# A three-block float32 network on one core: the turn between sublayers with six held weight units, eight unit buffers and five stream buffers

## The chip, the cores and the metric

The kernel runs on one core of one Trainium2 chip. The metric is the device time of one launch in microseconds (us), as the median of several runs.

## The reference

A residual stream `x` of 256 tokens by 1024 columns, float32, passes two adaLN-modulated blocks and one block of another kind. Cut to what matters:

```
for i in range(2):                       # block i: ffn(i,0), mixer, ffn(i,1)
    mod = silu(c) @ ada_w[i] + ada_b[i]
    x = sub(x, swiglu(ffn_w_in[i,0], ffn_w_out[i,0]))
    x = sub(x, pool_mixer) if i == 0 else sub(x, mla_mixer)
    x = sub(x, swiglu(ffn_w_in[i,1], ffn_w_out[i,1]))
# sub:  h = rmsnorm(x) * g * (1 + scale) + shift;  y = rmsnorm(fn(h)) * g';  x + w * (1 + gate) * y
h = rmsnorm(x)                           # second block
x = x + merged(attention, convolution, memory attention of h @ w_in) @ w_o
x = x + 2 of 32 experts for each token (w_up: 1024 x 512, w_down: 256 x 1024)
```

`swiglu` is `(silu(gate) * up) @ w_out` with `gate, up = h @ w_in` and an inner width of 2816, handled as 11 slices of 256.

## The kernel before, in words

The sublayers have numbers q: 0 is ffn(0,0), 1 the pool mixer, 2 ffn(0,1), 3 ffn(1,0), 4 the MLA mixer, 5 ffn(1,1); then the second block ("mix") and the experts. The 256 tokens are two tiles (t = 0, 1) of 128.

**Weights.** All weights come through one stream. SyncE (`stream`, L430) loads chunks of 1 MB into `NRAW` raw buffers in a fixed order. Chunk m waits until the chunk that lay in its buffer, m - NRAW, is done with: for most chunks until VectorE has split its last unit, for a few that TensorE reads unsplit (`ada_w`, `pool_w` and some of MLA) until TensorE has used them. A chunk has two units of 1024 columns. A unit is split into a high part `uh` (ScalarE, L449) and the rest `ul` (VectorE, L460), kept in `NUNIT` unit buffers; unit u waits until TensorE has used unit u - NUNIT. Both engines take their splits in program order with their other work: `split_high`/`split_low(upto)` emit every split up to a given unit that the raw buffers allow, and whatever is written behind them waits.

**Products.** A float32 product is three matmuls: high by high (L524), rest of the weight (L525), rest of the activation (L526). `linear` goes unit by unit over both tiles. `linear_by_tile` holds `held` units, does all of them for tile 0 and then for tile 1, so that tile 0 is complete earlier; `mid` is put ahead of one unit of tile 0.

**An FFN.** For each slice b, `up(b)` is 48 matmuls into two PSUM banks (banks 4 and 5, `AB`, from b = 1 on), ScalarE takes silu from a bank (`sg`, L1174), VectorE multiplies (`ug`, L1207) and thereby frees the bank, `spread(b)` (L1124) transposes `ug` in the middle of `up(b+1)`, ScalarE and VectorE make its high part and rest (`bh`, `bl`), and `outp(b)` is 24 matmuls into the y banks. The order on TensorE is up(b), outp(b-1), up(b+1), outp(b). In an FFN that ends in a turn, outp(9) and outp(10) are done last and together, by tile. Between these pieces VectorE adds up modulation columns of a later sublayer (L707, L710).

**The turn** (`edge_pe`, `edge_act`, `edge_dve`, `edge_roots_pool`) is used four times: 2 to 3, 3 to 4, 4 to 5, 5 to mix. When y of a tile is complete, VectorE multiplies it by the gain (L1077), ScalarE sums its squares (L802), GpSimd takes the root, VectorE updates x (L1085), ScalarE sums the squares of x, GpSimd takes the root, VectorE makes a diagonal matrix of it (L1091), TensorE multiplies the tile of x by it, which also turns it (L976, 8 matmuls), ScalarE applies scale and shift and rounds (L1038, L1042) and VectorE takes the rest `hl` (L1069), in four groups of 256 columns, g = 0 to 3. Then the first product of the next sublayer starts, by tile, with four units. `keep_busy` (L588) is four matmuls without use.

Of the kernel before, what the change touches and what calls it, by code (L numbers as in the profile page):

```python
# [8 lines left out]
F32R = mybir.dt.float32r  # L9
# [5 lines left out]
P = 128  # L15
T = 2
# [6 lines left out]
NRAW = 6  # L23
NUNIT = 6
# [129 lines left out]
def plan(I):  # L154
# [74 lines left out]
def build(nc, I, out_ap):  # L229
    ctx = ExitStack()  # L230
    with ctx:
# [24 lines left out]
        gT_l = [bl[:, 2 * i:2 * i + 2, :] for i in range(2)]  # L256
        sg = sb("sg", [P, T, 256])
# [294 lines left out]
        def linear_by_tile(pe, key, held, k0, K, lhi, llo, ready, banks, begin=True, mid=None, done=None,  # L552
                           mid_at=None):
# [416 lines left out]
        def edge_turn_pe(pe, q, t):  # L970
            pe.wait_ge(dve_done, tv("dg", q, t))
            for g in range(4):
# [6 lines left out]
                pe.frees(b, act_done, ta, "tf", q, t, g)  # L979
# [30 lines left out]
        def edge_pe(pe, s, q, key, banks, done):  # L1010

            keep_busy(pe, EDGE_BANKS[3], 4)
            edge_turn_pe(pe, q, 0)
            linear_by_tile(pe, key, 4, 0, KD, lh, ll, edge_ready(pe, q), banks,
                           mid=lambda: edge_turn_pe(pe, q, 1), mid_at=3, done=done)

        def edge_act(act, s, q, key, silu, scale, bias, more=True):
# [26 lines left out]

            y_squares(0)
# [20 lines left out]
        def edge_dve(dve, s, q, key, more=True):  # L1066
# [26 lines left out]

            gain(0, 1)
# [12 lines left out]
            low(0, 3)  # L1107
# [10 lines left out]
        def ffn_pe(pe, q, nb, up, down, ready, between, tail=None, begun=False, edge=False):  # L1118
# [10 lines left out]
            def outp(b, mid=None):  # L1129
                n = b % 2  # L1130
                if edge and b == nb - 1:
                    part = lambda v, k, t: v[(b - 1 + k // 2) % 2][:, k % 2, t * P:(t + 1) * P]
                    linear_by_tile(pe, ("fo",), 4, 0, 4, lambda k, t: part(gT_h, k, t),
                                   lambda k, t: part(gT_l, k, t),
                                   lambda k, t: pe.wait_ge(dve_done, tv("gl", q, b - 1 + k // 2)), YB, begin=False,
                                   mid=lambda: spread(b), mid_at=1, done=("y", q))
# [6 lines left out]
            for b in range(nb):  # L1143
# [6 lines left out]
                if b and not (edge and b == nb - 1):  # L1150
                    outp(b - 1, mid=(lambda: spread(nb - 1)) if b == nb - 1 else None)
# [5 lines left out]
        def ffn_act(act, q, nb, up, down, between, tail=None, begun=False, edge=False):  # L1157
            def spread(b):
                act.wait_ge(pe_done, tp("gT", q, b))
                if b >= 2:  # L1160
                    act.wait_ge(pe_done, tp("out", q, b - 2))
                act.e.activation(gT_h[b % 2][:, :, :], PB[6][:, :].rearrange("p (a b) -> p a b", b=S),  # L1162
                                 AF.Copy).then_inc(act_done, ta.put("gh", q, b))

            for b in range(nb):
# [12 lines left out]
                elif b:  # L1178
# [4 lines left out]
            if edge:  # L1183
                held_act(act, ("fo",), 4, 2)
# [3 lines left out]
        def ffn_dve(dve, q, nb, up, down, between, combine=False, tail=None, begun=False, edge=False):  # L1188
            def spread(b):
                n = b % 2  # L1190
# [5 lines left out]
            for b in range(nb):  # L1196
# [14 lines left out]
                elif b:  # L1211
# [4 lines left out]
            if edge:  # L1216
                held_dve(dve, ("fo",), 4, 2)
# [13 lines left out]
        def sub_ffn_pe(pe, i, s, between=nothing, tail=None):  # L1231
# [11 lines left out]
            else:  # L1243
# [3 lines left out]
                   side, tail, begun=q != 2, edge=q > 0)  # L1247
# [23 lines left out]
        def sub_ffn_dve(dve, i, s, between=nothing, tail=None):  # L1271
# [11 lines left out]
            else:  # L1283
                edge_dve(dve, q - 1, q, up_key(i, s)(0))
# [642 lines left out]
        def mla_pe(pe):  # L1927
# [69 lines left out]
            out_unit(2)  # L1997
            three(7)
            for k in range(3, KD - 4):
                out_unit(k)  # L2000
            linear_by_tile(pe, ("mo",), 4, KD - 4, KD, lh, ll, ready, YB, begin=False, done=("y", 4))
            edge_frees(pe, 4)

        def mla_act(act):
# [33 lines left out]
            units_act(act, ("mo",), KD - 4)  # L2038
            held_act(act, ("mo",), 4, 2)

        def mla_dve(dve):
            edge_dve(dve, 3, 4, ("mi",), more=False)
# [41 lines left out]
            units_dve(dve, ("mo",), KD - 4, mid=last_pairs, mid_k=0)  # L2084
            held_dve(dve, ("mo",), 4, 2)
# [542 lines left out]
        def mix_dve(dve):  # L2628
# [7 lines left out]
            for n, (nm, _, _) in enumerate(PROJ):  # L2636
                if n == 0:
                    edge_dve(dve, 5, "mix", ("pj",))
# [808 lines left out]
```

## Time and profile before

| | |
|---|---|
| median of 3 runs | 1566.01 us (1565.28 to 1566.88) |
| profiled execution | 1568.05 us, of which the span of the trace is 1565.8 us |
| mean granted clock of TensorE | 0.993 |
| TensorE busy | 97% of the span |
| VectorE busy | 78% |
| ScalarE busy | 56% |
| GpSimd busy | 7% |
| read from HBM | 371.39 MB |

In a row of a timeline the first number is the start in us from the span's start, the second the duration, "x5" says that five such instructions in a row are shown as one, and a bracket at the end says how long the engine sat idle before and which instruction released it. Matmuls of 512 columns start 0.23 us apart, though each is shown with about 0.39 us, since they overlap.

### The profile page before, as it was taken

What the parts mean: (1) busy time and instruction counts of PE and PEld (TensorE: products, weight loads), DVE (VectorE), ACT (ScalarE), POOL (GpSimd) and SP (SyncE); (2) the same over time, 40 slices, a digit from 0 to 9 for tenths busy, and PEclk for the clock granted to TensorE, in tenths of its full rate; (3) what the DMA queues carried; (4) which work ended last, traced back from release to release, by engine and by line L of the source; (5) the groups of instructions that cost most, each with busy time, mean ns of one, the idle gap of its engine ahead of it and who ended that gap; (6) DMA issues with size and microseconds to landing.
All of it is one profiled execution on the core that took longest, in us unless ns stands there. A gap on an engine that the chain in (4) does not pass through costs nothing.

```text
span 1565.8 us, 19135 instructions
## 1 busy us (share of the span) xinstructions
PE 1520.5 (97%) x7373; PEld 1213.7 (78%) x7373; DVE 1214.8 (78%) x1774; ACT 882.1 (56%) x1357; POOL 115.5 (7%) x176
## 2 busy tenths in 40 slices
PE   6999999999999999999999999999999999999998
PEld 3878876887877887776788887777788888787876
DVE  1898978888867888655586654669888798988996
ACT  3545436544437444476564544655567477776774
POOL 1110020000002000015211000000001000000000
PEclk9999999999999999999999999899999999999999
DMA  9999856998857988333287544445323469989993
GB/s 345 373 378 348 303 206 213 319 315 294 308 173 268 327 295 298 136 109 108 82 295 203 167 163 135 163 143 194 113 89 124 168 248 359 348 315 327 324 338 134
DMA packets 196401, 373.75 MB, mean 239 GB/s; under 512 B 9042, under 2 KB 102672, under 8 KB 196304
## 3 DMA queue, kind: packets, MB, share of 16 engines
q1 hardware_dynamic: 176688, 301.08, 55.7%
q0 software_dynamic: 18928, 69.77, 12.7%
q10 hardware_dynamic: 688, 1.62, 0.3%
q8 instruction: 60, 0.98, 0.2%
q14 instruction: 37, 0.30, 0.1%
HBM read 371.39 MB, written 1.05 MB: 238 GB/s over the span
## 4 chain that ended last, share of the span: by engine, by line
PE 88%; ACT 4%; DVE 4%; DMA 1%; POOL 1%; issue 1%; SPq 0%; DVEq 0%; ACTq 0%
PE banks L524 26%; PE banks L526 25%; PE banks L525 25%; PE banks L1124 1%; ACT arena L802 1%; DVE ul L460 1%; ACT uh L449 1%; PE banks L2361 1%; DMA raw<-in_ffn_w_in 1%; PE banks L2963 1%; PE banks L1970 1%; PE banks L761 1%; ACT full L1038 1%; DMA raw<-in_ada_w 1%; PE banks L1795 1%
## 5 line engine op out<-in xcount | busy, mean ns | idle before, releaser
L460 DVE TENSOR_TENSOR ul<-raw,uh 128x1024 fp32r<-128x1024 f32 (+2 forms) x548 | 656.9, 1209 | 148.9 <-ACT uh L449 139.7
L449 ACT ACTIVATE uh<-raw 128x1024 fp32r<-128x1024 f32 (+2 forms) x548 | 568.4, 1048 | 347.8 <-PE banks L526 341.6
L524 PE MATMUL banks<-uh,hh 128*128 128x512 f32 (+2 forms) x1296 | 517.7, 399 | 13.0 <-DVE hl L1069 6.4
L526 PE MATMUL banks<-uh,hl 128*128 128x512 f32 (+2 forms) x1296 | 504.7, 389 | 0.0
L525 PE MATMUL banks<-ul,hh 128*128 128x512 f32 (+2 forms) x1296 | 503.2, 388 | 0.0
L524 PEld LDWEIGHTS banks<-uh,hh 128*128 128x128 f32 x1296 | 244.8, 189 | 72.2 <-DVE hl L1069 10.1
L526 PEld LDWEIGHTS banks<-uh,hl 128*128 128x128 f32 x1296 | 244.8, 189 | 51.4
L525 PEld LDWEIGHTS banks<-ul,hh 128*128 128x128 f32 x1296 | 245.3, 189 | 45.8 <-issue 0.2
L524 PE MATMUL banks<-uh,bh 128*128 128x512 f32 x512 | 207.2, 405 | 1.0 <-DVE bl L3160 0.9
L526 PE MATMUL banks<-uh,bl 128*128 128x512 f32 x512 | 200.1, 391 | 0.0
L525 PE MATMUL banks<-ul,bh 128*128 128x512 f32 x512 | 199.6, 390 | 0.0
L710 DVE SCALAR_TENSOR_TENSOR arena<-arena,sc 128x512 f32<-128x512 f32 x210 | 157.9, 752 | 9.5
L524 PEld LDWEIGHTS banks<-uh,bh 128*128 128x128 f32 x512 | 96.1, 188 | 29.2 <-DVE bl L3160 6.2
L526 PEld LDWEIGHTS banks<-uh,bl 128*128 128x128 f32 x512 | 96.1, 188 | 20.9
L525 PEld LDWEIGHTS banks<-ul,bh 128*128 128x128 f32 x512 | 96.3, 188 | 20.0 <-issue 1.7
L686 POOL DMA_DIRECT2D arena<-in_ada_w x60 | 45.2, 755 | 480.7 <-DVE arena L710 402.0
L1174 ACT ACTIVATE sg<-banks 128x256 f32<-128x256 f32 x88 | 29.0, 380 | 62.0 <-PE banks L526 62.0
L2344 DVE SCALAR_TENSOR_TENSOR Gs<-arena,Gs 128x256 f32<-128x256 f32 x88 | 42.7, 485 | 3.1
L1207 DVE TENSOR_TENSOR ug<-sg,banks 128x256 f32<-128x256 f32 x88 | 32.9, 414 | 11.4 <-ACT sg L1174 11.4
L1069 DVE TENSOR_TENSOR hl<-full,hh 128x256 fp32r<-128x256 f32 x32 | 13.6, 424 | 27.5 <-ACT hh L1042 27.5
L1192 DVE TENSOR_TENSOR bl<-banks,bh 128x512 fp32r<-128x512 f32 x44 | 30.1, 683 | 4.1 <-ACT bh L1162 4.1
L769 ACT ACTIVATE arena<-banks 128x128 f32<-128x128 f32 x20 | 5.5, 278 | 40.6 <-PE banks L746 40.6
(392 smaller groups left out, 1270.8 us busy)
## 6 DMA issues: line engine op xcount, KB each, us to landing
raw<-in_ffn_w_in SPq DMA_DIRECT2D x176, 512.0 KB, 6.6
raw<-in_w_up SPq DMA_DIRECT2D x64, 1024.0 KB, 7.1
arena<-in_ada_w POOLq DMA_DIRECT2D x60, 1024.0 KB, 6.6
raw<-in_ffn_w_out SPq DMA_DIRECT2D x44, 1024.0 KB, 5.5
raw<-in_w_down SPq DMA_DIRECT2D x32, 1024.0 KB, 7.0
raw<-in_w_in SPq DMA_DIRECT2D x22, 1024.0 KB, 5.0
raw<-in_ada_w SPq DMA_DIRECT2D x12, 1024.0 KB, 11.0
raw<-in_w_mem_kv SPq DMA_DIRECT2D x4, 1024.0 KB, 6.5
```

What stands on the lines that cost most here:

```text
L449: act.e.activation(uh[r][:, 0:w], raw[m % NRAW][:, h * w:(h + 1) * w], AF.Copy).then_inc(act_done, ta.put("hi", u))
L460: dve.e.tensor_tensor(ul[r][:, 0:w], raw[m % NRAW][:, h * w:(h + 1) * w], uh[r][:, 0:w].bitcast(F32), ALU.subtract).then_inc(dve_done, tv. ...
L524: pe.e.matmul(o, a, wh, start=k + j == s0, stop=False)
L525: pe.e.matmul(o, a, wl, start=False, stop=False)
L526: mm = pe.e.matmul(o, b, wh, start=False, stop=k + j == s1)
L686: pool.e.dma_start(ada_raw[m % NADA], v).then_inc(ada_ring[m % NADA], 16)
L710: dve.e.scalar_tensor_tensor(buf, w, sc[:, k:k + 1], buf, ALU.mult, ALU.add).then_inc(dve_done, tv.put())
L761: pe.e.matmul(PB[b], ones[:, :], buf, start=True, stop=True).then_inc(pe_done, tp.put("ada_t", old))
L1174: act.e.activation(sg[:, t, :], PB[up_banks(b)[t]][:, 0:256], AF.Silu).then_inc(act_done, ta.put("silu", q, b, t))
L1192: dve.e.tensor_tensor(gT_l[n][:, :, :], PB[6][:, :].rearrange("p (a b) -> p a b", b=S), gT_h[n][:, :, :].bitcast(F32), ALU.subtract).then_inc(
L1207: mul = dve.e.tensor_tensor(o, sg[:, t, :], u, ALU.mult)
L2344: tap = dve.e.scalar_tensor_tensor(y, u, w, y, ALU.mult, ALU.add)
```

## The change

- `NRAW` goes from 6 to 5, `NUNIT` from 6 to 8.
- In the FFNs that end in a turn (q = 2, 3, 5) outp(8), outp(9) and outp(10) are done last and together, by tile, with six held units. outp(8) no longer stands between up(9) and up(10). The weights stream in that order. Slice 10 has buffers of its own (`ch`, `cl`). In MLA six units instead of four are held for the output product.
- The turn's TensorE work for tile 0 goes ahead of the last held unit of tile 1's y. That for tile 1 goes ahead of tile 1's first product; it stood ahead of tile 0's last unit. `keep_busy` is gone from the turn.
- VectorE takes scale and shift of group 1 of tile 0, and ScalarE's and VectorE's work of the turn is in another order.
- The program is built with a DMA scratch of 4096 bytes (`dynamic_dma_scratch_size=4096`).

```diff
@@
-NRAW = 6
-NUNIT = 6
+NRAW = 5
+NUNIT = 8
@@ the stream's order, ffn(i, s)
-            if b:
+            if b and not (i + s and b >= NFF - 2):
                 wide(("fo", i, s, b - 1), I["ffn_w_out"][i, s], (b - 1) * 256)
-        wide(("fo", i, s, NFF - 1), I["ffn_w_out"][i, s], (NFF - 1) * 256)
+        for b in range(NFF - 3, NFF) if i + s else (NFF - 1,):
+            wide(("fo", i, s, b), I["ffn_w_out"][i, s], b * 256)
@@ linear_by_tile
+                    if late is not None and (t, i) == (1, held - 1 if late_at is None else late_at):
+                        late()
@@ edge_pe
-            keep_busy(pe, EDGE_BANKS[3], 4)
-            edge_turn_pe(pe, q, 0)
-            linear_by_tile(pe, key, 4, 0, KD, lh, ll, edge_ready(pe, q), banks,
-                           mid=lambda: edge_turn_pe(pe, q, 1), mid_at=3, done=done)
+            linear_by_tile(pe, key, 4, 0, KD, lh, ll, edge_ready(pe, q), banks, done=done,
+                           late=lambda: edge_turn_pe(pe, q, 1), late_at=0)
@@ edge_act
+            high(0, 0)
+            second_high()
+            high(0, 2)
             y_squares(1)
-            high(0, 0)
-            high(0, 1)
+            high(0, 3)
             x_squares(1)
-            high(0, 2)
-            high(0, 3)
@@ edge_dve
+            diagonal(0)
+            split_low(dve, dve.unit_at + 3)
+            second_scaled()
+            low(0, 0)
+            low(0, 1)
             gain(1, 1)
-            diagonal(0)
             gain(1, 0)
-            low(0, 0)
+            low(0, 2)
             update(1)
-            low(0, 1)
-            split_low(dve, dve.unit_at + 3)
-            low(0, 2)
+            low(0, 3)
             diagonal(1)
-            low(0, 3)
@@ ffn_pe
-                    linear_by_tile(pe, ("fo",), 4, 0, 4, lambda k, t: part(gT_h, k, t),
+                    linear_by_tile(pe, ("fo",), 6, 0, 6, lambda k, t: part(gT_h, k, t),
...
-                if b and not (edge and b == nb - 1):
+                if b and not (edge and b >= nb - 2):
                     outp(b - 1, mid=(lambda: spread(nb - 1)) if b == nb - 1 else None)
@@ mla_pe
-            out_unit(2)
-            three(7)
-            for k in range(3, KD - 4):
-                out_unit(k)
-            linear_by_tile(pe, ("mo",), 4, KD - 4, KD, lh, ll, ready, YB, begin=False, done=("y", 4))
+            linear_by_tile(pe, ("mo",), 6, KD - 6, KD, lh, ll, ready, YB, begin=False, mid=lambda: three(7), mid_at=1,
+                           done=("y", 4), late=lambda: edge_turn_pe(pe, 5, 0))
```

The order of instructions on two engines, at the places of which the prediction speaks:

On TensorE, sublayer 2, at the end of up(9), before (`uh,bh` is a product with the activations of `outp`, `uh,hh` one of `up`):

```order
L525 MATMUL banks<-ul,hh 128x512
L526 MATMUL banks<-uh,hl 128x512
L524 MATMUL banks<-uh,bh 128x512
L525 MATMUL banks<-ul,bh 128x512
L526 MATMUL banks<-uh,bl 128x512
```

and of the change:

```order
L528 MATMUL banks<-ul,hh 128x512
L529 MATMUL banks<-uh,hl 128x512
L527 MATMUL banks<-uh,hh 128x512
L528 MATMUL banks<-ul,hh 128x512
L529 MATMUL banks<-uh,hl 128x512
```

The first product of up(10) now directly follows the last of up(9); both write banks 4 and 5.

On VectorE, the turn from 2 to 3 from the gain of tile 1 on, before:

```order
L1077 TENSOR_TENSOR arena<-banks,Gs 128x512
L1091 TENSOR_SCALAR arena<-ident,st 128x128
L1077 TENSOR_TENSOR arena<-banks,Gs 128x512
L1069 TENSOR_TENSOR hl<-full,hh 128x2x128
L1085 SCALAR_TENSOR_TENSOR x<-arena,st,x 128x512 x2
L1069 TENSOR_TENSOR hl<-full,hh 128x2x128
L460 TENSOR_TENSOR ul<-raw,uh 128x1024
L1069 TENSOR_TENSOR hl<-full,hh 128x2x128
L1091 TENSOR_SCALAR arena<-ident,st 128x128
L1069 TENSOR_TENSOR hl<-full,hh 128x2x128 x5
L460 TENSOR_TENSOR ul<-raw,uh 128x1024 x5
L1207 TENSOR_TENSOR ug<-sg,banks 128x256 x2
```

and of the change:

```order
L1102 TENSOR_SCALAR arena<-ident,st 128x128
L463 TENSOR_TENSOR ul<-raw,uh 128x1024
L1108 TENSOR_SCALAR full<-banks,ab 128x128 x2
L1080 TENSOR_TENSOR hl<-full,hh 128x2x128 x2
L1088 TENSOR_TENSOR arena<-banks,Gs 128x512 x2
L1080 TENSOR_TENSOR hl<-full,hh 128x2x128
L1096 SCALAR_TENSOR_TENSOR x<-arena,st,x 128x512 x2
L1080 TENSOR_TENSOR hl<-full,hh 128x2x128
L1102 TENSOR_SCALAR arena<-ident,st 128x128
L1080 TENSOR_TENSOR hl<-full,hh 128x2x128 x4
L463 TENSOR_TENSOR ul<-raw,uh 128x1024 x7
L1229 TENSOR_TENSOR ug<-sg,banks 128x256 x2
```

Tile 0's diagonal and first two rests come ahead of tile 1's gain, and seven splits instead of five stand ahead of `ug` of the first slice.

On VectorE, output projection of the second block (the last `hl` are groups 2 and 3 of its input), before:

```order
L2440 TENSOR_TENSOR arena<-arena,banks 128x512 x2
L2445 TENSOR_TENSOR arena<-arena 128x512 x2
L460 TENSOR_TENSOR ul<-raw,uh 128x1024 x6
L853 TENSOR_TENSOR hl<-banks,hh 128x512 x2
L460 TENSOR_TENSOR ul<-raw,uh 128x1024 x3
```

and of the change:

```order
L2460 TENSOR_TENSOR arena<-arena,banks 128x512 x2
L2465 TENSOR_TENSOR arena<-arena 128x512 x2
L463 TENSOR_TENSOR ul<-raw,uh 128x1024 x8
L858 TENSOR_TENSOR hl<-banks,hh 128x512 x2
L463 TENSOR_TENSOR ul<-raw,uh 128x1024 x3
```

Eight splits instead of six stand ahead of the two `hl`. At the start of the experts the same happens ahead of the second expert's `ug` (L3180): seven instead of five.

## Rows read from the trace of the kernel before

**Rows 1.** The page, parts 1 and 6: engine busy us, share, count; DMA issues

```profile
PE 1520.5 (97%) x7373; PEld 1213.7 (78%) x7373; DVE 1214.8 (78%) x1774; ACT 882.1 (56%) x1357; POOL 115.5 (7%) x176
...
raw<-in_w_up SPq DMA_DIRECT2D x64, 1024.0 KB, 7.1
...
raw<-in_w_in SPq DMA_DIRECT2D x22, 1024.0 KB, 5.0
...
raw<-in_w_mem_kv SPq DMA_DIRECT2D x4, 1024.0 KB, 6.5
```

**Rows 2.** Timeline of PE, turn 2 to 3: start us, duration, line, [idle <-releaser]

```profile
468.71 0.39 PE L524 MATMUL banks<-uh,bh 128*128 128x512 f32 x1
...
483.51 1.95 PE L976 MATMUL banks<-arena,x 128*128 128x128 f32 x16
485.21 0.47 PE L524 MATMUL banks<-uh,hh 128*128 128x512 f32 x1
...
492.12 0.39 PE L524 MATMUL banks<-uh,hh 128*128 128x512 f32 x1
...
497.56 0.60 PE L1124 MATMUL banks<-ident,ug 128*128 128x128 f32 x4
```

**Rows 3.** Timeline of DVE, the same turn

```profile
474.96 0.28 DVE L1091 TENSOR_SCALAR arena<-ident,st 128x128 f32<-128x128 f32 x1
...
485.44 0.43 DVE L1069 TENSOR_TENSOR hl<-full,hh 128x256 fp32r<-128x256 f32 x1 [2.35 <-ACT hh L1042]
...
489.83 5.76 DVE L460 TENSOR_TENSOR ul<-raw,uh 128x1024 fp32r<-128x1024 f32 x5 [0.52 <-ACT uh L449]
495.51 0.74 DVE L1207 TENSOR_TENSOR ug<-sg,banks 128x256 f32<-128x256 f32 x2
```

**Rows 4.** Timeline of all engines, end of up(9) of sublayer 2

```profile
443.94 0.39 PE L524 MATMUL banks<-uh,bh 128*128 128x512 f32 x1
...
445.48 0.74 DVE L1207 TENSOR_TENSOR ug<-sg,banks 128x256 f32<-128x256 f32 x2
```

**Rows 5.** Timeline of all engines, end of up(9) of sublayer 3

```profile
643.89 0.39 PE L524 MATMUL banks<-uh,bh 128*128 128x512 f32 x1
...
645.15 0.74 DVE L1207 TENSOR_TENSOR ug<-sg,banks 128x256 f32<-128x256 f32 x2
```

**Rows 6.** Timeline of all engines, end of up(9) of sublayer 5

```profile
943.52 0.39 PE L524 MATMUL banks<-uh,bh 128*128 128x512 f32 x1
...
944.21 0.75 DVE L1207 TENSOR_TENSOR ug<-sg,banks 128x256 f32<-128x256 f32 x2 [0.83 <-ACT sg L1174]
```

**Rows 7.** Timeline of all engines, pool sublayer, first part

```profile
245.96 0.37 SPq L430 DMA_DIRECT2D raw<-in_w_mem_kv  x1
245.98 2.00 ACT L449 ACTIVATE uh<-raw 128x1024 fp32r<-128x1024 f32 x2
...
247.06 1.23 DVE L460 TENSOR_TENSOR ul<-raw,uh 128x1024 fp32r<-128x1024 f32 x1 [0.40 <-ACT uh L449]
```

**Rows 8.** Timeline of all engines, pool sublayer, later part

```profile
262.37 2.35 DVE L460 TENSOR_TENSOR ul<-raw,uh 128x1024 fp32r<-128x1024 f32 x2
...
265.90 1.23 DVE L932 TENSOR_TENSOR arena<-banks,Gs 128x1024 f32<-128x1024 f32 x1 [1.18 <-PE banks L1520]
```

**Rows 9.** Timeline of all engines, output projection of the second block

```profile
1222.90 6.89 DVE L460 TENSOR_TENSOR ul<-raw,uh 128x1024 fp32r<-128x1024 f32 x6
...
1229.72 1.28 DVE L853 TENSOR_TENSOR hl<-banks,hh 128x512 fp32r<-128x512 f32 x2
...
1231.52 0.39 PE L524 MATMUL banks<-uh,hh 128*128 128x512 f32 x1
```

**Rows 10.** Timeline of all engines, start of the experts

```profile
1272.35 0.47 DVE L3180 SCALAR_TENSOR_TENSOR ug<-sg,arena,banks 128x256 f32<-128x256 f32 x1
...
1273.94 0.38 PE L3062 MATMUL banks<-ident,ug 128*128 128x128 f32 x2
```

**Rows 11.** One window of PE: us, busy, PEclk, DMA share, GB/s

```profile
980.00:994.00 14.00, 13.45 (x64) 0.63 0.46 164
```

More of the change, by code:

```diff
@@ L552, in linear_by_tile @@
         def linear_by_tile(pe, key, held, k0, K, lhi, llo, ready, banks, begin=True, mid=None, done=None,
-                           mid_at=None):
+                           mid_at=None, late=None, late_at=None):
             got = [take_unit(pe, key) for _ in range(held)]
@@ L1043, in high, with second_high @@
                     act_done, ta.put("th", q, t, g))
+            def second_high():
+                act.wait_ge(dve_done, tv("tf", q, 0, 1))
+                act.e.activation(edge_columns(hh, 0, 1), edge_part(0, 1), AF.Copy).then_inc(
+                    act_done, ta.put("th", q, 0, 1))
             y_squares(0)
@@ L1064, in edge_act, with edge_dve @@
                 split_high(act, act.unit_at + NUNIT - 2)
-        def edge_dve(dve, s, q, key, more=True):
+        def edge_dve(dve, s, q, key, scale, bias, more=True):
             def low(t, g):
@@ L1092, in diagonal, with second_scaled @@
                     dve_done, tv.put("dg", q, t))
+            def second_scaled():
+                dve.wait_ge(pe_done, tp("T", q, 0, 1))
+                for k in range(2):
+                    dve.e.tensor_scalar(edge_part(0, 1)[:, k, :], PB[EDGE_BANKS[1]][:, k * P:(k + 1) * P], scale(2 + k),
+                                        bias(2 + k), ALU.mult, ALU.add).then_inc(dve_done, tv.put())
+                tv.same("tf", q, 0, 1)
             gain(0, 1)
@@ L1116, in up_banks, with slot, ffn_pe @@
             return AB if b else (YB[0][0], YB[0][1])
-        def ffn_pe(pe, q, nb, up, down, ready, between, tail=None, begun=False, edge=False):
+        def slot(edge, nb, b):
+            return 2 if edge and b == nb - 1 else b % 2
+        def ffn_pe(pe, q, nb, up, down, ready, between, tail=None, begun=False, edge=False, turn=None):
             def spread(b):
@@ L1131, in outp @@
                 if edge and b == nb - 1:
-                    part = lambda v, k, t: v[(b - 1 + k // 2) % 2][:, k % 2, t * P:(t + 1) * P]
-                    linear_by_tile(pe, ("fo",), 4, 0, 4, lambda k, t: part(gT_h, k, t),
+                    part = lambda v, k, t: v[slot(edge, nb, b - 2 + k // 2)][:, k % 2, t * P:(t + 1) * P]
+                    linear_by_tile(pe, ("fo",), 6, 0, 6, lambda k, t: part(gT_h, k, t),
                                    lambda k, t: part(gT_l, k, t),
-                                   lambda k, t: pe.wait_ge(dve_done, tv("gl", q, b - 1 + k // 2)), YB, begin=False,
-                                   mid=lambda: spread(b), mid_at=1, done=("y", q))
+                                   lambda k, t: pe.wait_ge(dve_done, tv("gl", q, b - 2 + k // 2)), YB, begin=False,
+                                   mid=lambda: spread(b), mid_at=2, done=("y", q), late=turn)
                     return
@@ L1177, in ffn_act @@
                     spread(b)
-                elif b:
+                elif b and not (edge and b == nb - 2):
                     units_act(act, down(b - 1), 2, mid=(lambda: spread(nb - 1)) if b == nb - 1 else None)
@@ L1210, in ffn_dve @@
                     spread(b)
-                elif b:
+                elif b and not (edge and b == nb - 2):
                     units_dve(dve, down(b - 1), 2, mid=(lambda: spread(nb - 1)) if b == nb - 1 else None)
@@ L1246, in sub_ffn_pe @@
             ffn_pe(pe, q, NFF, up_key(i, s), down_key(i, s), edge_ready(pe, q) if q >= 3 else parts_ready(pe, q),
-                   side, tail, begun=q != 2, edge=q > 0)
+                   side, tail, begun=q != 2, edge=q > 0,
+                   turn=(lambda: edge_turn_pe(pe, "mix" if q == 5 else q + 1, 0)) if q else None)
             if q:
@@ L2037, in mla_act @@
             pair_heads_act(act, MLA)
-            units_act(act, ("mo",), KD - 4)
-            held_act(act, ("mo",), 4, 2)
+            units_act(act, ("mo",), KD - 6)
+            held_act(act, ("mo",), 6, 2)
         def mla_dve(dve):
-            edge_dve(dve, 3, 4, ("mi",), more=False)
+            edge_dve(dve, 3, 4, ("mi",), *modulated(4), more=False)
             for t in range(T):
@@ L2637, in mix_dve @@
                 if n == 0:
-                    edge_dve(dve, 5, "mix", ("pj",))
+                    edge_dve(dve, 5, "mix", ("pj",), lambda k: col("g_mix_2", k), lambda k: 0.0)
                     dve.e.memset(uT[:, :, 0:30], 0.0).then_inc(dve_done, tv.put("u0"))
```

25 lines of the change are left out of this document (15 added, 10 removed).

## The prediction, made before the changed kernel was run

> **What bounds the kernel now.** I read the page's shares first, then TensorE's timeline at each place that the change touches, then the engines that it waits for there. TensorE is busy 97% of the span [rows 1]: what counts is only what makes TensorE wait. Splits, loads and statistics are free where a product covers them. The reader is to look, place by place, at which wait of TensorE ends last.
>
> At the turn from 2 to 3, tile 1 of y starts at 468.71 and the first product of slice 1 at 492.12 [rows 2], 23.41 us. In them lie 24 matmuls of y, 48 of up(0) and two turns. Thirty matmuls from 485.21 to 492.12 make 0.23 each, and a turn takes 1.70 (483.51 to 485.21) [rows 2]. 72 x 0.23 + 2 x 1.70 = 20.0. So 3.4 us are lost: by `keep_busy`, waits for `hl` and the start of the pipeline. With four turns some 13.8 us are the most that closing the gaps could bring. Note how thin the cover is elsewhere: `ug` of the first slice is done at 496.25 and TensorE asks for it at 497.56 [rows 2, 3].
>
> **The change part by part.**
>
> *The turns.* Call 468.71 A. Tile 0's diagonal is done at 475.24, A + 6.5 [rows 3]. TensorE now has 36 matmuls of tile 1's y from A on, and 30 of them take 6.9: tile 0's turn follows without a wait, then the last 6, and y of tile 1 is complete at A + 10.0. The chain from y complete to the diagonal was 6.5 for tile 0, and tile 1's is the same chain; so its diagonal comes at A + 16.5, and TensorE has done tile 0's 24 products by then (6.9 + 1.7 + 30 x 0.23 = 15.5, plus waits for `hl` that I estimate at 0.8). Tile 1's turn starts at X' = A + 16.5. Before, it started at X = 483.51, and its first `hl` was done at 485.87, X + 2.4 [rows 2, 3]; then six products stood between, now none do. So tile 1's products start at X' + 2.4 = A + 18.9 and up(1) at A + 24.4. Of that, 12 matmuls (2.8) came over from outp(8): 21.6 against 23.4, a gain of 1.8. It can be 0 at worst and 3.4 at best. 4 to 5 is alike: 1.8. 3 to 4 has products of 416 columns, which cover less of the chain: I take 1.0. 5 to mix has 72-column products, where the chain alone sets the time, at a low clock (0.63 granted over 980 to 994 [rows 11]): 0.2. Near the end of each FFN outp(9) now has twelve matmuls more ahead of spread(10), which closes small gaps; I put 0.5 on all. **Gains: 1.8 + 1.8 + 1.0 + 0.2 + 0.5 = 5.3.**
>
> *up(10) directly behind up(9).* Both use banks 4 and 5, and the bank is free only when `ug` of slice 9 has read it. Outp(8), 24 matmuls or 5.5 us, covered that. TensorE now wants the bank where outp(8) started: 443.94, 643.89 and 943.52. `ug` starts at 445.48, 645.15 and 944.21 [rows 4 to 6], in the first two behind two additions of modulation columns on VectorE (L710). Its first half takes about 0.4 (0.74 for both): waits of 2.0, 1.7 and 1.1. Nothing hides them; behind the matmul stands all of TensorE. **Loss 4.8**, bounds 3.3 (if the additions slip behind `ug`) and 6.
>
> *Seven splits ahead of `ug` behind a turn.* Five took from 489.83 to 495.51, 1.14 each [rows 3]. Two more end `ug` at 498.5, X + 15.0. TensorE asks for it 48 matmuls (11.0) behind the first product of tile 1, X' + 2.4 + 11.0 = X' + 13.4. **Loss 1.6 in each of 2 to 3 and 4 to 5, 3.2.** If the two extra splits are found done earlier it is 0. The other two turns have no such `ug`.
>
> *Eight ahead of `hl` in the output projection.* Six took from 1222.90 to 1229.72, and the first `hl` was done at 1230.4; TensorE reached its product at 1231.52 [rows 9]. Two more make it 1232.7: **loss 1.2.**
>
> *Seven ahead of `ug` at the experts' start.* It starts at 1272.35, so 1274.6 now, done at 1275.1; its spread is at 1273.94 [rows 10]: **loss 1.2.** In the steady run of an FFN or of the experts ScalarE waits for TensorE to free a unit, and two more buffers bring nothing there.
>
> *Five raw buffers.* The look-ahead of raw and units together stays nearly the same (6 + 3 chunks against 5 + 4), and a split chunk is asked for at the same product. It is otherwise behind an unsplit chunk. In the pool sublayer the second half of `w_mem_kv` is loaded as chunks 48 and 49. Chunk 49 waited for the first `ada_w` chunk, 43, and was issued at 245.96 [rows 7]. Now chunk 48 waits for chunk 43, and goes at 245.96; the kind lands 6.5 us later by the median [rows 1], at 252.5. But ScalarE wants it at 245.98 [rows 7], ahead of the scaled x for the pooling, and VectorE at 247.06. Both then run 6.5 late, through the pooling chain on VectorE. That chain ended with slack on TensorE's side, but the splits that began at 262.37 and took 2.35 now stand right ahead of y's gain, which began at 265.90 [rows 8]: 262.37 + 6.5 + 2.35 = 271.2, 5.3 late, less about 0.5 of waits on ScalarE further down the chain that vanish. x, the next splits, the remaining products of `w_mem_kv` and the next turn all follow. **Loss 4.8.** By the medians of other loads of 1 MB, 5.0 (`w_in`) and 7.1 (`w_up`) [rows 1], it would be 3.3 to 5.4.
>
> The Trainium skill ("DMA: Bandwidth & Descriptors", section on the anatomy of one DMA) gives 2.0 us plus bytes by 436 GB/s, which would be 4.4 for 1 MB. The trace's 6.5 disagrees; by the page's figure this loss would be 2.7 and the whole 2.1 less. I go by the row.
>
> *The rest.* The DMA scratch touches only GpSimd's issues, which run ahead of need; MLA's shifted work has some tenths of slack left. Both at nothing.
>
> **Sum.** -5.3 + 4.8 + 3.2 + 1.2 + 1.2 + 4.8 = +9.9. The profiled execution of before took 1568.05 (span 1565.8 and 2.25 around it), 2.0 over the median of 1566.01. So 1577.9 when profiled and **1575.9** as a median.
>
> **The rivals.** A change under 0.2% (3.1 us) can't be told from none.
>
> *The gaps close fully and the clock stays up: faster.* If the diagonals come with the matmuls that cover them, the turns return 13.8 rather than 4.8. The last turn alone decides whether the clock stays up: 14 us at 0.63 cost 14 x 0.37 = 5.2 against full speed [rows 11]. 1575.9 - 9.0 - 5.2 = 1561.7. For it: TensorE is fed from y straight into the turn. Against: tile 1's chain of 6.5 starts only when y is whole, and only 30 matmuls and a turn are there to cover it. It decides from the point at which tile 1's diagonal is ready before A + 15.5. Chance 0.14.
>
> *The gaps close, the clock doesn't:* 1575.9 - 9.0 = 1566.9, the same. Chance 0.14.
>
> *The pool sublayer hides its load,* because ScalarE's split of chunk 48 isn't where I put it: 1575.9 - 4.8 = 1571.1. Chance 0.14.
>
> *The change isn't felt:* waits move within a stage and nothing adds up, 1566. Chance 0.05.
>
> *The stream becomes a bound among the experts:* units are split two units earlier against the same load, 12 matmuls or 2.8 us where one tile is done, and the loads of `w_up` take 7.1 [rows 1]; if ten of them then miss by 0.6, that adds 6 (an assumed number of misses): 1581.9. Chance 0.08.
>
> **How the numbers follow.** My forecast has 0.45, with its own range of 1571 to 1581. Slower by over 0.2%: 0.45 + 0.14 + 0.08 = 0.67. Same: 0.14 + 0.05 = 0.19. Faster: 0.14. The range of 8 in 10 goes from 1561 to 1582.
>
> **What would show it right or wrong.** Right: a wait of 1 to 2 us of L527 for `ug` at the end of up(9), three times; waits of the spread for `ug` right behind two turns; ScalarE idle for about 6 us ahead of a split in the pool sublayer for a DMA, and the following turn 5 us late; `hl` of the second block's output projection late by 1.2. In the turn from 2 to 3, no wait at tile 0's turn and one at tile 1's. Wrong: chunk 48 landed before ScalarE came to it; or a turn shorter by 3 us. The likeliest error is a stall that I count in full and that another takes over, since several of them follow each other on one engine.

## The result, and the profile after

The changed kernel took 1584.13 us (median, 1579.81 to 1587.68, 6 runs) against 1565.65 of before (1564.79 to 1569.67, 6 runs). The ratio is 1.0112, 95% interval 1.0097 to 1.0126: 1.1% slower, beyond the end of the predicted range (1582) and nearly twice as far from before as forecast, +18.5 instead of +9.9. The profiled execution took 1582.93, with a span of 1580.7.

The page after, first and sixth part, against [rows 1]:

```profile
PE 1518.5 (96%) x7341; PEld 1211.0 (77%) x7341; DVE 1216.2 (77%) x1782; ACT 878.7 (56%) x1349; POOL 115.0 (7%) x176
...
raw<-in_w_up SPq DMA_DIRECT2D x64, 1024.0 KB, 7.2
...
raw<-in_w_mem_kv SPq DMA_DIRECT2D x4, 1024.0 KB, 6.1
```

TensorE is busy for 2 us less, in a span that is 14.9 longer. Some 4 us of the busy time of before was the turns' `keep_busy`, which is gone. Up to the last 20 us of the span TensorE ran at half clock for 20.5 us in either trace, at other places. So between these two executions the clock comes to nothing in sum, and the loss is waiting. A wait is told here in two ways: "idle" is the number in a row's bracket, and a "gap" is the time between the starts of two matmuls less the usual 0.23, some 0.15 more than idle. The list of what TensorE waited for, over the whole span (releaser, us idle in total, times, longest):

```profile
PE banks L527 <- DVE hl L1080: 6.2, 8, 1.8
...
PE banks L527 <- DVE ug L1229: 4.4, 3, 1.8
PE banks L527 <- DVE ul L463: 3.6, 3, 2.7
PE banks L527 <- DVE bl L1214: 3.6, 4, 1.7
PE banks L2983 <- ACT arena L2976: 3.2, 3, 2.2
...
PE banks L1146 <- DVE ug L1229: 2.9, 2, 1.5
...
PE banks L527 <- DVE hl L858: 1.1, 1, 1.1
PE banks L3082 <- DVE ug L3200: 1.1, 1, 1.1
```

Four of these waits were named beforehand: L527 for `ug` three times (the bank of up(9)), the spread L1146 for `ug` twice (behind a turn), `hl` L858 (output projection) and L3082 for `ug` (second expert). Two were not: L527 for `bl`, 3.6 in four, and L2983 for ScalarE's `arena`, 3.2, of which 1.6 was there before (as L2963).

The turn from 2 to 3 on TensorE after, against [rows 2]:

```profile
473.45 0.39 PE L527 MATMUL banks<-uh,bh 128*128 128x512 f32 x1
...
480.25 1.94 PE L981 MATMUL banks<-arena,x 128*128 128x128 f32 x16
...
488.23 0.50 PE L527 MATMUL banks<-uh,hh 128*128 128x512 f32 x1 [0.56 <-DVE hl L1080]
...
490.16 2.05 PE L981 MATMUL banks<-arena,x 128*128 128x128 f32 x16 [0.28 <-DVE arena L1102]
492.68 0.50 PE L527 MATMUL banks<-uh,hh 128*128 128x512 f32 x1 [0.47 <-DVE hl L1080]
...
498.26 0.39 PE L527 MATMUL banks<-uh,hh 128*128 128x512 f32 x1
```

Tile 1's y starts at 473.45 and the first product of slice 1 at 498.26, 24.8 later, of which 2.8 are the twelve matmuls that came over from outp(8): 22.0, where it was 23.4. Tile 0's turn at 480.25 waits for nothing, tile 1's at 490.16 for its diagonal, and the product behind it for `hl`, as forecast.

TensorE at the end of up(9), the first product of up(10), against [rows 4]:

```profile
450.18 0.51 PE L527 MATMUL banks<-uh,hh 128*128 128x512 f32 x1 [1.84 <-DVE ug L1229]
```

VectorE there, and in the turn and behind it, against [rows 3, 4]:

```profile
449.72 0.74 DVE L1229 TENSOR_TENSOR ug<-sg,banks 128x256 f32<-128x256 f32 x2
...
496.59 8.04 DVE L463 TENSOR_TENSOR ul<-raw,uh 128x1024 fp32r<-128x1024 f32 x7 [0.52 <-ACT uh L452]
504.55 0.74 DVE L1229 TENSOR_TENSOR ug<-sg,banks 128x256 f32<-128x256 f32 x2
...
511.37 0.68 DVE L1214 TENSOR_TENSOR bl<-banks,bh 128x512 fp32r<-128x512 f32 x1
```

Seven splits in a row stand ahead of `ug`, which is done at 505.3. TensorE's spread comes with a gap of 1.65 for it. The `bl` of the same slice follows at 511.37, and outp(0) comes with a gap of 0.8 for it.

### The profile page after: what moved, and what is told of

The parts are those of the page before. It is cut to its first block, busy times and chain, and to the rows that moved or that the text cites. A ratio compares the mean times of both kernels' runs of the same rounds, so it can differ in the third digit from the quotient of the medians.

```text
span 1580.7 us, 19003 instructions
## 1 busy us (share of the span) xinstructions
PE 1518.5 (96%) x7341; PEld 1211.0 (77%) x7341; DVE 1216.2 (77%) x1782; ACT 878.7 (56%) x1349; POOL 115.0 (7%) x176
## 4 chain that ended last, share of the span: by engine, by line
PE 77%; DVE 12%; ACT 5%; DMA 3%; POOL 1%; issue 1%; SPq 0%; DVEq 0%; ACTq 0%
PE banks L527 22%; PE banks L529 22%; PE banks L528 22%; DVE ul L463 6%; DMA raw<-in_ffn_w_in 2%; ACT uh L452 2%; DVE arena L715 1%; PE banks L1146 1%; PE banks L2381 1%; PE banks L2983 1%; ACT arena L807 1%; ACT full L1044 1%; PE banks L1993 1%; DMA raw<-in_ada_w 1%; DMA raw<-in_w_up 1%
## 5 line engine op out<-in xcount | busy, mean ns | idle before, releaser
L527 PE MATMUL banks<-uh,hh 128*128 128x512 f32 (+2 forms) x1296 | 518.2, 400 | 18.0 <-DVE hl L1080 6.2
L527 PEld LDWEIGHTS banks<-uh,hh 128*128 128x128 f32 x1296 | 245.2, 189 | 78.2 <-DVE hl L1080 8.2
L527 PE MATMUL banks<-uh,bh 128*128 128x512 f32 x488 | 197.1, 404 | 4.5 <-DVE bl L1214 3.6
L529 PE MATMUL banks<-uh,bl 128*128 128x512 f32 x488 | 190.9, 391 | 0.0
L528 PE MATMUL banks<-ul,bh 128*128 128x512 f32 x488 | 190.3, 390 | 0.0
L527 PEld LDWEIGHTS banks<-uh,bh 128*128 128x128 f32 x488 | 91.7, 188 | 30.4 <-DVE bl L1214 5.3
L529 PEld LDWEIGHTS banks<-uh,bl 128*128 128x128 f32 x488 | 91.6, 188 | 20.0
L528 PEld LDWEIGHTS banks<-ul,bh 128*128 128x128 f32 x488 | 91.9, 188 | 18.8 <-issue 1.4
L1146 PE MATMUL banks<-ident,ug 128*128 128x128 f32 x176 | 26.6, 274 | 3.0 <-DVE ug L1229 2.9
L1146 PEld LDWEIGHTS banks<-ident,ug 128*128 128x128 f32 x176 | 21.5, 140 | 10.4 <-DVE ug L1229 4.3
```

Of the source, the lines that this page charges most:

```text
L527: pe.e.matmul(o, a, wh, start=k + j == s0, stop=False)
L528: pe.e.matmul(o, a, wl, start=False, stop=False)
L529: mm = pe.e.matmul(o, b, wh, start=False, stop=k + j == s1)
L1146: mm = pe.e.transpose(PB[6][:, f * S + t * P:f * S + (t + 1) * P], ug[b % 2][:, t, f * P:(f + 1) * P], ident[:, :])
```

## The experiments

Shifts "between two points" are differences of the start of the same TensorE instruction in two traces. Where runs of one kernel spread over 10 us and more, the place in the trace is read rather than the median. The experiments ran on several chips, each beside runs of the kernel before, whose median there was 1565.2 to 1566.7; a difference of two experiments from different chips is uncertain by about 1 us for that.

### e1_sizes: the buffers alone

```diff
-NRAW = 6
-NUNIT = 6
+NRAW = 5
+NUNIT = 8
...
-    nc = _bacc.Bacc("TRN2", target_bir_lowering=False, num_devices=1)
+    nc = _bacc.Bacc("TRN2", target_bir_lowering=False, num_devices=1, dynamic_dma_scratch_size=4096)
```

> The kernel before with five raw buffers, eight unit buffers and the DMA scratch of 4096 bytes, and nothing else of the change. Theory P (the loss is made by single waits whose places the trace of the change shows, and most of them come from the two extra splits that stand ahead of other work): the load wait in the pool sublayer 3.5, the two extra splits behind three FFN starts 5, output projection 1.3, experts 4, start 1 to 2, so 1580 to 1582 against 1565.7. Rival T (the new turn and the missing outp(8) make the loss): within 3 us of 1565.7.

1577.99 us (1575.64 to 1586.58, 5 runs), ratio 1.0073 (1.0051 to 1.0095). Rival T falls: the sizes alone cost 11 to 12 of the change's 18.5. They cost less than P had summed up, which was 1580 to 1582. The slowest of its runs was the profiled one, 8.6 above the median, so its trace is not typical of the kernel. It shows a wait at the start larger than P's 1 to 2:

```profile
62.68 2.00 ACT L449 ACTIVATE uh<-raw 128x1024 fp32r<-128x1024 f32 x2 [7.44 <-DMA raw<-in_ffn_w_in]
64.59 0.58 ACT L1162 ACTIVATE bh<-banks 128x512 fp32r<-128x512 f32 x1
...
66.22 0.64 ACT L1174 ACTIVATE sg<-banks 128x256 f32<-128x256 f32 x2
```

ScalarE stands 7.44 us at a split whose chunk has not landed, and behind it in program order stand `bh` of slice 0 and `sg` of slice 1. TensorE idles 4.5 for `bl`, and runs at half clock around it. In one window of TensorE (us, busy, granted clock, DMA share, GB/s), 60 to 80 of this kernel:

```profile
60.00:80.00 20.00, 15.53 (x57) 0.83 1.04 352
```

The kernel before has 20.00 busy at 1.00 in the same window, and about the same load on the DMA (371 GB/s).

### e2_look6: splits counted ahead as with six buffers

```diff
+LOOK = 6
...
-                split_high(act, min(cap, act.unit_at + NUNIT - 1))
+                split_high(act, min(cap, act.unit_at + LOOK - 1))
```

and so in the other places of `units_act`, `units_dve`, `edge_act` and `edge_dve` that count units ahead; the eight buffers stay.

> The change with its eight unit buffers, but the number of splits that units_act, units_dve and the end of the turn emit ahead is counted as with six buffers. Theory P: the waits for ug, bl and hl behind bursts of splits go, and ScalarE no longer waits for landings ahead of other work at the experts' start: 10 to 12 us less than the change, 1572 to 1574. The pool wait and the bank waits at up(10) stay. Rival S (the five raw buffers starve the stream everywhere): at most 3 less than the change, above 1581.

1569.86 us (10 runs), ratio 1.0024 (1.001 to 1.0038): 14.3 less than the change (13.8 by the two ratios), more than P said, and far from rival S. The count of splits emitted ahead is the main cause. The waits of the spread for `ug`, of `hl` L858 and of L3082 are gone from the list:

```profile
PE banks L528 <- DVE hl L1081: 5.7, 7, 1.8
...
PE banks L528 <- DVE ul L464: 4.2, 3, 2.7
PE banks L528 <- DVE ug L1230: 3.8, 3, 1.7
...
PE banks L2984 <- ACT arena L2977: 1.6, 3, 0.5
```

The ten runs lie within 6.5 us, 1567.18 to 1573.68, where the change's six spread over 8 and e1's five over 11. The thirteen of the kernel before on that chip spread over 8.1, though, so a spread alone shows little.

### e12_turn_splits: only the splits behind the turn

```diff
-                split_high(act, act.unit_at + NUNIT - 2)
+                split_high(act, act.unit_at + 4)
...
-                split_low(dve, dve.unit_at + NUNIT - 2)
+                split_low(dve, dve.unit_at + 4)
```

> The change, with only the splits right behind a turn's held units cut from seven to five (edge_act and edge_dve); everywhere else splits are counted ahead as with eight buffers. Theory P: the waits of the spread for ug (1.65 and 1.6) and of outp for bl (0.8 and 0.8) behind two turns go, 4.9 less than the change's 1584.1: 1579. The other 9 or so of e2's 14 come from the start, the output projection and the experts. Rival: all of e2's gain is here, 1570 to 1572; or the waits only shift one slice on, 1584.

1591.6 us (1588.04 to 1596.44, 4 runs), ratio 1.0156: slower than the change by 7.5. P's number was wrong. The second rival has the mechanism, though its 1584 was too low as well: the wait moves one slice on and grows.

```profile
503.53 5.77 DVE L463 TENSOR_TENSOR ul<-raw,uh 128x1024 fp32r<-128x1024 f32 x5 [0.53 <-ACT uh L452]
509.21 0.74 DVE L1229 TENSOR_TENSOR ug<-sg,banks 128x256 f32<-128x256 f32 x2
509.88 3.49 DVE L463 TENSOR_TENSOR ul<-raw,uh 128x1024 fp32r<-128x1024 f32 x3
513.28 0.48 DVE L712 TENSOR_SCALAR arena<-arena,sc 128x512 f32<-128x512 f32 x1
...
518.31 0.68 DVE L1214 TENSOR_TENSOR bl<-banks,bh 128x512 fp32r<-128x512 f32 x1
```

`ug` is now in time, but as the rest of the kernel still counts eight ahead, the splits that were left out come as three in a row behind `ug`, and with them the modulation additions and `bl` come later. TensorE:

```profile
519.05 0.50 PE L527 MATMUL banks<-uh,bh 128*128 128x512 f32 x1 [2.33 <-DVE bl L1214]
```

2.33 idle for `bl`, where the change had 0.63, and half clock behind it; the turn and its follow-up come out 1.6 dearer than in the change, two times. The start weighs more. The profiled execution, 11.7 longer than the change's, had lost 8.4 of that by 98 us (TensorE busy 15.80 of the 20 us from 60 to 80, at a clock of 0.83), in code that is the same as the change's: see below.

### e3_outp8: four held units instead of six

```diff
-            if b and not (i + s and b >= NFF - 2):
+            if b:
                 wide(("fo", i, s, b - 1), I["ffn_w_out"][i, s], (b - 1) * 256)
...
-                    linear_by_tile(pe, ("fo",), 6, 0, 6, lambda k, t: part(gT_h, k, t),
+                    linear_by_tile(pe, ("fo",), 4, 0, 4, lambda k, t: part(gT_h, k, t),
```

> The change with outp(8) back between up(9) and up(10) in the FFNs, so that four units are held there instead of six; turn order, buffers and MLA as in the change. Theory P: the bank waits of 2.0, 1.7 and 1.2 and the stretch at half clock behind the first go (6.5 in all), tile 0's turn waits about 1 at three turns but tile 1's chain starts earlier by as much: 5 to 7 less than the change, 1577 to 1579. Rival H (holding six units is what pays for the turn): slower than the change.

1589.13 us (4 runs), ratio 1.0143: 5 slower than the change where P said 5 to 7 faster. Rival H is right. The bank waits are gone, and this stands in their place:

```profile
480.66 2.05 PE L980 MATMUL banks<-arena,x 128*128 128x128 f32 x16 [2.34 <-DVE arena L1101]
...
490.69 2.05 PE L980 MATMUL banks<-arena,x 128*128 128x128 f32 x16 [0.27 <-DVE arena L1101]
```

Tile 0's turn goes ahead of the last of four units, when only 18 matmuls of tile 1's y have run, and waits 2.34 for a diagonal that comes 6.5 after tile 0's y. That happens at three turns: 7.5 us of gaps instead of 4.9 of bank waits, 2.6 more. The last turn also ran at half clock for 17 us, against 10 in the change, and the whole trace up to its last 20 us for 30.7 against 20.5, which costs about 5 us. These are the two parts of the 7.4 that the profiled executions differ by, and no run shows how much of the second the edit brings.

### e9_four_held: the same without the other losses

> e6_look_pool with outp(8) back between up(9) and up(10) and four units held in the FFNs. Theory C (twelve more matmuls of tile 1's y cover the chain to tile 0's diagonal; without them the turn waits 2.5 three times, as in e3's trace, for which the bank waits of 4.9 are the price): 2.6 for the waits and 2 or so more of half clock slower than e6_look_pool, 1568 to 1570. Rival B (the bank wait is the dearer of the two once the splits are out of the way): faster than e6_look_pool.

1570.07 us (6 runs) against 1564.30 of e6_look_pool below: 5.8 slower. The two profiled executions differ by 3.5, with half clock for 20.5 us in both: the three turns wait 7.0 for their diagonals in place of 3.8 for the bank. The other 2.3 of the medians stand in neither trace. So six held units pay for the bank waits that they bring, with the splits out of the way too.

### e4_pool: the pool sublayer's split moved

```diff
-            split_high(act, act.unit_at + 1)
             ada_copy_act(act, ADA_POOL[0], POOL_BANKS[0], START_BUFS[0])
             for g in range(4):
...
                 ta.same("tf", 1, g)
+            split_high(act, act.unit_at + 1)
             ada_copy_act(act, ADA_POOL[1], POOL_BANKS[1], START_BUFS[1])
```

On VectorE the matching split goes between the pooling of groups 1 and 2.

> The change with the split of the second w_mem_kv chunk moved in the pool sublayer: on ScalarE behind the eight scaled copies of x for the pooling, on VectorE between the pooling of groups 1 and 2. Theory P: ScalarE's wait of 5.5 for the load hides nothing any more, 3 to 4 less than the change, 1580 to 1581. Rival: the wait was hidden and the time stays at 1584.

1584.33 us, but over 1576.52 to 1590.58 in 4 runs: the median says nothing. The traces do. ScalarE in the change, then here:

```profile
251.57 2.00 ACT L452 ACTIVATE uh<-raw 128x1024 fp32r<-128x1024 f32 x2 [5.54 <-DMA raw<-in_w_mem_kv]
...
254.16 3.75 ACT L1487 ACTIVATE arena<-banks,ab 128x256 f32<-128x256 f32 x8
```

```profile
247.79 3.75 ACT L1486 ACTIVATE arena<-banks,ab 128x256 f32<-128x256 f32 x8 [0.46 <-PE banks L835]
251.52 2.00 ACT L452 ACTIVATE uh<-raw 128x1024 fp32r<-128x1024 f32 x2
```

The eight scaled copies start at 247.79 instead of 254.16 and the split behind them no longer waits. Against the kernel before, the turn behind the pool sublayer is 2.97 late in the change and 0.56 early here: 3.5. Of that 0.7 was there ahead of the sublayer, so these two traces give the wait 2.8. Those of e2_look6 and e6_look_pool, which differ by the same edit, give it 4.3: the product there that TensorE waits for with `ul` starts at 276.87 and 274.40, though e6_look_pool had come to the sublayer 1.8 later.

### e5_scratch: the DMA scratch alone

> The kernel before with the DMA scratch of 4096 bytes and nothing else. Theory P: GpSimd's loads of modulation weights have time to spare, 1565 to 1567. Rival: the smaller scratch holds GpSimd's issues up and with them the additions on VectorE, 2 us or more slower.

1566.79 us (10 runs), ratio 1.0007 (0.9997 to 1.0017): nothing that can be told.

### e6_look_pool: both together

> e2_look6 and e4_pool together: the change, splits counted ahead as with six buffers, and the pool sublayer's split moved. Theory P: the two are independent, e2's 1569.9 less the 3.5 that e4's trace shows between the pool sublayer's start and its turn: 1566 to 1567, level with the kernel before. Rival: another wait takes the place of the pool wait, 1569 to 1570.

1564.3 us (10 runs), ratio 0.999 (0.9979 to 1.0002): 5.6 less than e2_look6, where P said 3.5; against the kernel before on its own chip each time it is 4.3. Taking away one cause leaves the other's gain in place, and with both removed the change is level with the kernel before.

### e7_sizes_look: the buffers with the old turn

> The kernel before with five raw buffers, eight unit buffers, the small scratch, and the splits counted ahead as with six: everything of the change about buffers, with the old turn and outp(8) in its old place. Theory P: only the pool wait is left of the loss, and the experts run some 2 to 3 shorter as in e2's trace: 1566 to 1568. The turn with six held units is then worth e2's 1569.9 less this, about nothing or a small loss, since its bank waits (4.9) eat its gains (about 5). Rival: the turn gains by itself, and this is above 1572.

1567.88 us (10 runs), ratio 1.0017 (1.0007 to 1.0027). It keeps the pool wait, as e2_look6 does, which is 2.0 slower, or 0.8 against the kernel before on its own chip each time. So the new turn with six held units, its bank waits in, is worth about nothing or a small loss, as P said.

### e8_slip and e11_slip_again: `ug` ahead of the additions

```diff
-                    units_dve(dve, up(b), KD, mid=(lambda b=b: spread(b - 1)) if b else None)
+                    if edge and b == nb - 2:
+                        units_dve(dve, up(b), KD - 2, mid=lambda b=b: spread(b - 1), mid_k=KD // 2)
+                        dve.rate, rate = 0, dve.rate
+                        units_dve(dve, up(b), 2)
+                        dve.rate = rate
+                    else:
+                        units_dve(dve, up(b), KD, mid=(lambda b=b: spread(b - 1)) if b else None)
...
+                if edge and b == nb - 2:
+                    dve.later.go(dve.rate)
```

so that the additions (`dve.later`) come behind `ug` of that slice. The rest is as in e6_look_pool.

> e6_look_pool, and at the end of up(9) VectorE does ug of slice 9 ahead of the two modulation additions. Theory P: the bank waits of 2.0 and 1.7 fall to about 1.2, and no half clock follows the first: 1.3 to 3 less than e6_look_pool. Rival: the wait goes to what follows the additions, and the time stays.

> e8_slip once more, beside e10_busy on the same chip and with more rounds: 1561 to 1564 by theory P, 2 to 3 below the kernel before. If it is level with the kernel before, the gain seen in e8_slip was noise.

1562.65 us (10 runs), ratio 0.9984 (0.9973 to 0.9994), and again 1564.19 (12 runs), ratio 0.9986 (0.9978 to 0.9995). The first is 1.6 below e6_look_pool, on the same chip; the second is only level with it, and 1.0 below the kernel before by the medians, where P said 2 to 3. In the traces the three bank waits are 3.1 idle in all where e6_look_pool had 3.8: only the second fell, from 1.65 to 1.02, as the first was down to 1.02 already. e6_look_pool, then e8_slip:

```profile
PE banks L528 <- DVE ug L1230: 3.8, 3, 1.6
```

```profile
PE banks L528 <- DVE ug L1236: 3.1, 3, 1.1
```

This version is faster than the change, and by 0.15% faster than the kernel before, which is at the edge of what can be told. What its own step adds to e6_look_pool is 0 to 1.6 us.

### e10_busy: matmuls without use in the last turn

```diff
+                           mid=lambda: keep_busy(pe, EDGE_BANKS[3], 6 if q == "mix" else 0), mid_at=3,
```

> e8_slip with six matmuls without use ahead of the last unit of tile 0 in the turn to the second block, where TensorE otherwise waits 2.0 for hl. Theory K (the short 72-column products and these waits are what brings the clock down for 13 us there, and filling a wait keeps it up): 3 to 6 less than e8_slip. Rival: the clock goes by more than this gap, the time stays within 1 us of e8_slip, or rises by what the six matmuls take beyond the wait.

1563.7 us (12 runs) beside e8's second measurement, 1564.19 on the same chip: within 0.5. Windows of TensorE, e8_slip and then this:

```profile
976.00:992.00 16.00, 15.30 (x64) 0.57 0.30 101
```

```profile
976.00:992.00 16.00, 14.18 (x67) 0.79 0.38 130
```

The clock there rose from 0.57 to 0.79, and the turn came out 1.0 us shorter between the same two TensorE instructions of the two traces, where 6.8 us less at half clock would be 3.4 if TensorE alone set the time. Idle time took its place (busy 14.18 instead of 15.30): in this turn the chain of VectorE and ScalarE sets much of the time, at either clock. Then another stretch of half clock stands among the small products ahead of the experts, which e8_slip's trace has not, and costs 1.6. Windows there, e8_slip and then this:

```profile
1240.00:1256.00 16.00, 14.65 (x112) 1.00 0.01 2
```

```profile
1240.00:1256.00 16.00, 14.66 (x99) 0.89 0.01 2
```

So theory K is right that filling a wait keeps the clock up in this turn, and wrong in the price. Whether the later stretch comes from the edit or by chance one trace can't show.

## Why the prediction was wrong

The direction held, with the chance of 0.67 on it. The size did not. By its own steps:

- *The turns, gain 4.8.* 2 to 3 gained 1.4 (forecast 1.8). For the others the shift over a turn less the waits known there gives 1.1 for 3 to 4 (1.0), 1.2 for 4 to 5 (1.8) and 1.1 for the last (0.2). Together 4.8. Right in sum. Of the 0.5 for small gaps the shifts show 0.2 at most.
- *up(10) behind up(9), loss 4.8.* Gaps of 2.0, 1.7 and 1.2 against 2.0, 1.7 and 1.1. Right. But behind the first the clock fell, for 450.5 to 453.9: 0.57 granted over 450 to 454, 1.7 us more, and in no term. That is luck of the execution as well: in e12_turn_splits the same 1.84 idle had 1.00 around it. e3 and e9 show that with the order tried here the bank wait is the price for the turn's cover.
- *Seven splits ahead of `ug`, 3.2.* Gaps of 1.65 and 1.6. Right. But the step ended there, and this is the first half of what failed: the slice's `bl` was late too, by 0.8 behind each of the two turns and by 1.0 at the start of sublayer 2, whose first slice has the same seven splits: 2.6 in no term.
- *Output projection 1.2 and second expert 1.2.* 1.3 and 1.2. Right.
- *Pool sublayer, 4.8.* ScalarE waited 5.5 for the load (6.5 forecast), and the two pairs of traces at e4 give the wait 2.8 and 4.3; I take 3.5. Against the kernel before the shift is only 2.4 there, as that one ran at half clock for 3.4 us behind a wait in its place, and the change didn't. By the medians of e2_look6 and e6_look_pool it is 4.3 to 5.6. Right in kind, and right in size within what the runs can tell.
- *The load behind it.* It took from 246.56 to 251.57, where the split starts: 5.0, below the row's 6.5. The 4.4 of the prediction is by the formula of the Trainium skill, page "DMA: Bandwidth & Descriptors", section "Anatomy of one DMA — SWDGE (gpsimd) path". The page gives it for loads that GpSimd issues, and this one is SyncE's; GpSimd's own loads of 1 MB took 6.7 by the median of the change's page of the profile, so the formula came out low for them too.
- *The step that failed* is the pricing of the two extra splits. The prediction priced them as 2.3 us of VectorE ahead of the first instruction that they make late, and closed with "In the steady run of an FFN or of the experts ScalarE waits for TensorE to free a unit, and two more buffers bring nothing there". For the steady run it held: outside the pool sublayer the change's ScalarE waits for no landing (0.3 us or more) from 70 to 1294 and from 1306 on. But it was let stand for the starts too. The start of the kernel had no term at all, and at the start of the experts the load was only in a rival, at 0.08. Counted eight ahead, ScalarE comes there to a split before its chunk has landed, and what is behind it in its queue waits for the DMA. Among the experts of the change:

```profile
1294.51 1.06 ACT L452 ACTIVATE uh<-raw 128x1024 fp32r<-128x1024 f32 x1 [1.93 <-DMA raw<-in_w_up]
...
1299.64 1.06 ACT L452 ACTIVATE uh<-raw 128x1024 fp32r<-128x1024 f32 x1 [0.56 <-DMA raw<-in_w_down]
...
1302.34 2.01 ACT L452 ACTIVATE uh<-raw 128x1024 fp32r<-128x1024 f32 x2 [0.42 <-DMA raw<-in_w_up]
1305.05 1.06 ACT L452 ACTIVATE uh<-raw 128x1024 fp32r<-128x1024 f32 x1 [0.70 <-DMA raw<-in_w_up]
...
1306.28 0.17 ACT L2976 ACTIVATE arena<-banks 128x8 f32<-128x8 f32 x1
```

```profile
1306.50 3.10 PE L2983 MATMUL banks<-arena 128*128 128x128 f32 x16 [2.17 <-ACT arena L2976]
```

Four waits for landings, 3.6 in all; `arena` comes at 1306.28, and TensorE's L2983 waits 2.17 for it, with another stretch of half clock behind. The DMA is full there (share 1.04, 392 to 398 GB/s from 1291 to 1306), and five chunks in a row landed 9.2 to 9.7 after their issue, where those of the kernel before took 6.3 to 7.8 at this place. It is a race: e3, e4 and e12 lose it too (L2983 waits 1.8, 2.1 and 2.0), while e1_sizes, with the count at eight as well, waits 0.37 for a landing and has no late `arena`. That is the rival's mechanism, with 2 to 3 us where it had 6. From the second expert's spread to the second gather (1273.94 to 1296.89 in the kernel before) the change loses 3.4 beyond the 1.2 of the forecast, of which 1.2 comes back by the end. In the kernel before the chunks landed some 4 to 7 us before their splits there. At the start of the kernel a wait for a landing lets TensorE idle for `bl`: 1.7 in the change's profiled run, 4.2 and 4.5 in those of e12 and e1, where the clock is halved around it too. Those three kernels run the same code there.

  For the runs without a trace only the time and the mean granted clock of each are on record. The kernel before goes from 1561.24 at 0.996 to 1569.89 at 0.991, 8.7 us, and its clock accounts for about 8 of them: a mean lower by 0.005 is 15.7 us more at half clock, in which TensorE does the work of 7.8. The change goes from 1579.81 at 0.993 to 1587.68 at 0.990, 7.9 us, of which the clock accounts for about 5; e1_sizes from 1575.64 at 0.995 to 1586.58 at 0.991, 10.9 us, about 6. So with the count at eight something beside the clock varies from run to run. That it is the race with the DMA is argued, not shown.

The named terms came to 4.9 + 3.3 + 1.3 + 1.2 + 3.5 - 4.8 = +9.4, against +9.9 forecast. The missing ones are 2.6 for `bl`, 1.7 for the clock behind the bank wait, 2.2 net among the experts and 0.6 net at the start of the profiled run, less 1.5 for the half clock that the kernel before alone had behind the pool sublayer: +15.0, where the two profiled executions differ by 14.9. The agreement is closer than the terms deserve, as the pool's alone is uncertain by 0.7. The median is 1.2 above the change's profiled run, and the median of before 2.4 below its own; these 3.6 belong to no place. The half clock is a likely one for the 2.4: e5_scratch, which has the code of before, took 1561.53 when profiled and was at half clock for 6.8 us where before's trace has 20.5.

e2_look6 shows the whole family at once: with the count at six, 14.3 of 18.5 us go. With the pool split moved too, nothing of the loss is left, and e7 agrees: with the count at six the buffers cost 2 us or so (1567.88, with the pool wait still in). The count at six does not make the loads come earlier. Among e2_look6's experts the chunks land 0.1 to 5 us before their splits for long stretches, less than the 2.5 to 9 of the change's steady run; but ScalarE waits for none of them.

Open: whether the bank waits can be had back without giving up the cover, as a free bank for up(10) was not tried. And no run has the count at eight with six raw buffers, so how much of the late landings is owed to the loss of the sixth one is not known.

## What to carry to other kernels

More buffers and a deeper look-ahead are two changes, and a constant that sets both should be split before it is touched: the work emitted ahead stands in front of short work on which another engine waits, and it comes earlier to data that haven't landed. Where a count in an in-order queue changes, follow every instruction behind it for one more slice, not only the first that is late, since what is pulled away from one place comes up at the next (e12). A wait that an edit removes may have been the cover of another: price both. A sentence on the steady run says nothing of the starts: give each start a term of its own.

## What the runs showed of the hardware

- Whether half clock follows a wait of 1 to 2 us on TensorE differed from one execution to the next. The wait of 1.80 us for `sg` in MLA (L1818, L1795 before) had half clock within 2.4 us behind it in the traces of before, the change and e2_look6, and none in those of e1_sizes, e5_scratch and e8_slip. The 1.84 us at the end of up(9) had it in the change and not in e12_turn_splits. Two profiled executions of one kernel, e8_slip and e11_slip_again, took 1561.75 and 1568.34 with 13.7 and 23.9 us at half clock up to their last 20 us.
- Raising the granted clock from 0.57 to 0.79 over 16 us by filling a gap made that turn 1.0 us shorter, where VectorE and ScalarE set much of the time.
- In the change's trace, with the DMA at a share of 1.04 (392 to 398 GB/s) loads of 1 MB landed 9.2 to 9.7 us after their issue, one every 2.6 to 2.7; shortly before, with fewer under way, they took 4.7 to 5.4 (the change, start of the experts).
- Taking the DMA scratch down to 4096 bytes cost nothing measurable (ratio 1.0007) with 60 loads issued by GpSimd.
